# A hybrid decoder step on one core: parameters made earlier, tables on two engines, gates and norms interleaved with other work

## The chip, the cores and the metric

The kernel runs on one core of a Trainium2 chip. The metric is the device time of one execution in microseconds (us), lower is better; the time given is the median of several executions. TensorE (PE), VectorE (DVE), ScalarE (ACT), GpSimd (POOL) and SyncE (SP) each take their instructions in program order from a queue of their own and wait for each other through semaphores. SP here only issues DMA transfers.

## The reference, cut to what matters

One layer of a decoder with two mixers in parallel, for 2048 prompt tokens and 64 sample tokens (8 sequences of 8) that have 4096 past positions in pages.

```python
proj = rmsnorm(x, g_pre) @ w_in            # q, k, v, index queries and keys, index weights, u
# attention: each query attends to the 256 keys with the highest index score
s = einsum('bqhd,bld->bqhl', qi, ki) * 64 ** -0.5
score = einsum('bqhl,bqh->bql', relu(s), wi) * 4 ** -0.5
_, idx = lax.top_k(score, 256)
a_o = sparse_attend(q, take(k, idx), take(v, idx), valid)
# state space: 32 groups of 64 complex states, 16 channels each
dt = exp(log_dt); mag = exp(lr * dt)
ar, ai = mag * cos(li * dt), mag * sin(li * dt)      # decay a
h[t] = a * h[t - 1] + B(a) u[t]                      # a scan over time
y = Re(C h) + d_skip * u
z = gelu(y)
s_o = z * sigmoid(z @ w_glu + b_glu)                 # the GLU gates
# both joined, then the MLP
mix = concatenate([a_o, s_o]) @ w_out
x = x + rmsnorm(mix, g_post)
hdn = square(relu(rmsnorm(x, g_ffn_pre) @ w_up))
y = x + rmsnorm(hdn @ w_down, g_ffn_post)
```

The model's width is 1024, the hidden width 4096. All is fp32. The large products are made as three products of high and low parts.

## The kernel before, in words

The tokens form 17 tiles of 128: 16 of the prompt, one with the 64 sample tokens. The kernel has three stages, `project_inputs` (line 57), `state_space` (384) and `blend` (777). A stage begins when all engines have ended the one before.

**Projections.** For each tile ACT squares and splits x, PE makes four banks of 24 matmuls and the transposes of queries and keys, ACT evacuates them (L192 to L206), DVE and POOL turn them by their positions (L262 to L272, L287 to L295), and SP loads the next tile and stores the last. SP's loads of a tile stand ahead of its stores.

**State space.** SP issues ten parameter loads (L463 to L465), the page table (L466) and u (L459), then gathers pages of index keys into a dense buffer kidx_d (L452): 64 pages before the MT moves and 64 after them; POOL gathers the other 128. Each gather is one load of a page number into a register and one DMA. DVE makes the decay, its sine and cosine with ACT's functions, then three tables by complex products (L373 to L380, seven operations each): eight powers of B, nine of C, and T, the powers of the per-chunk decay, by doubling (L607 to L634). A chunk is 8 tokens, so that the scan runs over 272 columns. PE's banks come in a written order: the eight transposes of the B table (L727), eight banks KT (L734) that need both tables, 24 transposes of u (L742), 32 banks w (L749), 32 banks Y (L756 to L761), and 20 gates (L768). ACT evacuates each bank (L525). DVE regroups u for the transposes (L645, three copies) and adds to KT (L639). SP moves KT into the Toeplitz matrix MT by eight DMAs (L476) when KT is whole, loads the states h0 (L479), and goes on gathering. DVE scans (L662 to L684) in four parts, two halves of the groups by two parts of the tokens; each writes H, which the Y banks need. GELU(y) leaves as four transfers to yt_d (L484) and comes back in another order by 32 (L487), is multiplied by the gates on DVE (L707) and stored as so_d (L492).

**Blend.** All that is left is cut into units, and one list `plan` gives their order for all engines at once. The selection of keys (units S), attention (A), and the samples' part (SQ, SI, SF, SC, SS, SE, SV, SO) come from functions that give each unit a cost; `merge` puts a side list between the units of a main one in proportion to the costs. SF are the 32 steps of the samples' search for the 256th highest score: each compares 4104 scores with a trial, the upper half on DVE (L2160), the lower on ACT (L1817). Four groups g of 4, 4, 4 and 5 tiles then go through the feed units:

- W(g, h, i): the half h of the output projection of tile i (L1433), 
- M1(g, i) and M2(g, i): the two norms behind it, N(g, i) the transposes (L1441),
- U(g, j): the MLP's 16 upward banks (L1455), D(g, m, q): its downward banks (L1470), E(g): the last norm of all tiles of the group.

A norm is a chain: ACT squares and sums (L1668), DVE makes the mean (L1990), ACT the root (L1673), DVE the inverse by one Newton step (L46 to L54) and the scaling by it (L2007, L2014, L2020), POOL adds the residual (L1891, L1902), SP stores or loads tiles in DRAM (L1284, L1296, L1301). In M1 and M2 it runs for one tile at a time; in E all squares come first, one root for all, then all scalings. The two halves of a downward sum are added on ACT and POOL (`act`: L1710, L1876) or DVE (`dve`). The residual tiles of E are loaded (L1296) into the buffer of the upward weights and downward hidden values, UP, which the last D bank still reads, so that these loads wait for all D banks. Search and attention of group g+1 lie beside the feed units of group g; group 3 has nothing beside it.

```python
queued = [u for u in feed if u[0] not in ("M1", "M2")]
...
sum_by[key] = "act" if i % 2 or beside_search(u) else "dve"
```

## Time and profile before

| what | value |
| --- | --- |
| median of 3 executions | 4224.88 us |
| fastest and slowest of them | 4220.42 and 4229.5 us |
| the profiled execution | 4228.36 us |
| its span in the profile | 4226.6 us |
| PE busy | 3284.0 us, 78% |
| PE's weight loads | 2492.9 us, 59% |
| DVE busy | 2168.2 us, 51% |
| ACT busy | 1818.0 us, 43% |
| POOL busy | 1197.2 us, 28% |
| DMA traffic | 357.41 MB, mean 85 GB/s |
| chain of waits | PE 45%, DVE 17%, issue 9%, ACT 6%, POOL 3%, DMA 2% |

The profile is of one execution. Its span runs from the first to the last instruction; the execution's own time is a little longer. A busy time is the time in which an engine computed; issuing DMAs isn't counted. PEclk is the granted clock of TensorE as a share of full speed, where 0.50 is 1.2 GHz and 1.00 is 2.4 GHz; the engine also shows 0.50 where it has nothing to do. DMA is the busy share of the core's 16 DMA engines. The profile divides the time of a view by groups of instructions with the same line, engine and tiles: out<-in, their number, their busy time, the mean or the least, median and greatest duration in ns, and the idle time before them with what ended it. The chain of waits follows the work that ended last back in time.

The stages lie at 0 to 361 us (projections), 361 to 709 (state space), and 709 to 4226.6 (blend). In the blend, 800 to 920 is the samples' search, and the norms of the four groups lie at 1270 to 1367, 1945 to 2128, 2760 to 2941 and 3610 to 3718.

### The profile page before, as it was taken

How to read it: one execution, taken by the hardware profiler on the slowest of the kernel's cores; microseconds unless marked ns; L12 is line 12 of the kernel's file. 1: busy time of each engine (PE TensorE's matmuls, PEld its weight loads, DVE VectorE, ACT ScalarE, POOL GpSimd, SP SyncE). 2: the span in 40 equal slices, each digit the busy share in tenths (PEclk: the TensorE clock that was granted, in tenths of full speed). 3: DMA queues.
4: the chain of work that ended last, by engine and by line, in shares of the span. 5: the costliest groups of instructions: out<-in, count | busy, mean ns of one | idle time of the engine just before them, and what ended most of it. 6: DMA issues, size and time to landing. Idle time of an engine off the chain costs nothing.

```text
span 4226.6 us, 48124 instructions
## 1 busy us (share of the span) xinstructions
PE 3284.0 (78%) x15896; PEld 2492.9 (59%) x15896; DVE 2168.2 (51%) x4234; ACT 1818.0 (43%) x3043; POOL 1197.2 (28%) x1080
## 2 busy tenths in 40 slices
PE   7993535306774899987489999874899999789997
PEld 6882422103453677764367776642677778578886
DVE  4335661593236784347886333577783333533233
ACT  3221211541344654465564445755644444423332
POOL 1222400103200461145034113531471112234344
PEclk9996667657776999998789999986999999889998
DMA  4444245305422222112222111231231111422221
GB/s 143 133 135 133 57 90 144 110 1 152 136 72 87 72 86 75 50 63 95 88 86 81 57 38 53 76 123 54 79 98 51 53 36 50 168 75 75 65 75 68
DMA packets 180516, 357.41 MB, mean 85 GB/s; under 512 B 39051, under 2 KB 93581, under 8 KB 178317
## 3 DMA queue, kind: packets, MB, share of 16 engines
q1 hardware_dynamic: 170028, 333.35, 25.2%
q0 software_dynamic: 10240, 20.99, 1.7%
q8 instruction: 128, 2.10, 0.2%
q14 instruction: 120, 0.98, 0.1%
HBM read 294.44 MB, written 67.01 MB: 86 GB/s over the span
## 4 chain that ended last, share of the span: by engine, by line
PE 45%; DVE 17%; issue 9%; ACT 6%; POOL 3%; DMA 2%; SPq 2%; POOLq 0%; ACTq 0%; DVEq 0%
PE r L1455 13%; PE r L1470 12%; PE po L1519 6%; PE tr L1510 3%; PE sc L1498 3%; DVE junk_v_b L2097 2%; DVE trial_b L2049 2%; PE r L1433 2%; DVE up_b L1950 2%; POOL acc_b L1876 2%; DVE dn_b L1950 2%; PE sc L1497 1%; ACT junk_a_b L1757 1%; ACT hr_b L1668 1%; DVE score_b L2033 1%
## 5 line engine op out<-in xcount | busy, mean ns | idle before, releaser
L1470 PE MATMUL r<-dn_b,h_b 128*128 128x512 f32 x2880 | 747.6, 414 | 103.1 <-ACT part_b L1710 48.2
L1470 PEld LDWEIGHTS r<-dn_b,h_b 128*128 128x128 f32 x2880 | 558.8, 199 | 266.5 <-ACT part_b L1710 63.4
L1455 PE MATMUL r<-x_hi_b,up_b 128*128 128x512 f32 x2048 | 662.6, 397 | 13.9 <-DVE x_lo_b L1970 9.6
L1876 POOL TENSOR_TENSOR acc_b<-acc_b,part_b 128x512 f32<-128x512 f32 x358 | 496.3, 1406 | 559.5 <-ACT part_b L1710 559.4
L1757 ACT ACTIVATE junk_a_b<-score_b,trial_b 128x384 int8<-128x384 f32 (+13 forms) x266 | 348.0, 1308 | 367.5 <-DVE trial_b L2049 350.6
L1455 PEld LDWEIGHTS r<-x_hi_b,up_b 128*128 128x128 f32 x2048 | 390.0, 190 | 105.3 <-issue 12.1
L1455 PE MATMUL r<-x_lo_b,up_b 128*128 128x512 f32 x1024 | 403.2, 394 | 0.0
L1857 POOL TENSOR_TENSOR hr_b<-hr_b 128x512 f32<-128x512 f32 x128 | 142.2, 1111 | 835.1 <-ACT hr_b L1697 835.1
L1786 ACT ACTIVATE pT_b<-tr 128x512 f32<-128x512 f32 (+3 forms) x320 | 168.9, 528 | 392.3 <-PE tr L1510 392.1
L1710 ACT ACTIVATE part_b<-r 128x512 f32<-128x512 f32 x358 | 206.6, 593 | 260.8 <-PE r L1470 172.3
L1519 PE MATMUL po<-V_sb,pT_b 128*128 128x64 f32 x2176 | 314.0, 285 | 3.0 <-DVE o_b L2114 2.3
L1519 PEld LDWEIGHTS po<-V_sb,pT_b 128*128 128x128 f32 x2176 | 272.2, 194 | 68.1 <-issue 54.8
L2128 DVE CUSTOM_DVE_ANT_0 prob_b<-sc,mk_b,mx_b 128x512 f32<-128x512 f32 (+3 forms) x192 | 124.9, 651 | 351.6 <-PE sc L1498 351.0
L1950 DVE TENSOR_TENSOR dn_b<-raw_b,dn_b 128x1024 fp32r<-128x1024 f32 x120 | 167.1, 1392 | 267.0 <-ACT dn_b L1657 266.4
L1950 DVE TENSOR_TENSOR up_b<-raw_b,up_b 128x1024 fp32r<-128x1024 f32 x136 | 190.3, 1400 | 215.0 <-ACT up_b L1657 214.6
L2097 DVE TENSOR_SCALAR_CACHE_REDUCE junk_v_b<-score_b,trial_b 128x384 bf16<-128x384 f32 (+13 forms) x182 | 267.9, 1472 | 1.4
L1865 POOL TENSOR_TENSOR h_b<-hr_b,h_b 128x512 fp32r<-128x512 f32 x128 | 224.2, 1751 | 149.1 <-ACT h_b L1721 149.1
L1455 PEld LDWEIGHTS r<-x_lo_b,up_b 128*128 128x128 f32 x1024 | 195.5, 191 | 38.9
L1792 ACT ACTIVATE prob_b<-prob_b,nmx_b 128x128 f32<-128x128 f32 (+15 forms) x128 | 153.9, 1203 | 139.9 <-DVE nmx_b L2134 139.9
L2128 DVE CUSTOM_DVE_ANT_0 prob_b<-sc,mk_b 128x512 f32<-128x512 f32 (+3 forms) x128 | 82.1, 641 | 241.2 <-PE sc L1498 230.3
L2049 DVE SCALAR_TENSOR_TENSOR trial_b<-trial_b,turn_b 128x1 int32<-128x1 int32 x434 | 183.3, 422 | 15.0
L1581 PE MATMUL r<-kv_b,qz_b 128*64 128x512 f32 x128 | 51.4, 891 | 178.0 <-DVE sbest_b L2189 157.3
(369 smaller groups left out, 6063.5 us busy)
## 6 DMA issues: line engine op xcount, KB each, us to landing
raw_b<-w_up SPq DMA_DIRECT2D x128, 512.0 KB, 3.9
raw_b<-w_down SPq DMA_DIRECT2D x128, 512.0 KB, 3.6
kv_b<-kv_pages SPq DMA_DIRECT2D x128, 128.0 KB, 2.9
kv_b<-kv_pages POOLq DMA_DIRECT2D x128, 128.0 KB, 3.0
raw_b<-w_out SPq DMA_DIRECT2D x64, 256.0 KB, 2.9
x_tok_sb<-x_all SPq DMA_DIRECT2D x17, 512.0 KB, 4.0
xT_sb<-xT_all SPq DMA_DIRECT2D x17, 512.0 KB, 4.6
kic_b<-kidx_d SPq DMA_DIRECT2D x4, 2048.0 KB, 13.7
```

What stands on the lines that cost most here:

```text
L1455: mm = pe.matmul(x[:, 0:w], wt[:, c], y[:, k], start=k == n == 0, stop=(k, n) == (KD - 1, 2))
L1470: mm = pe.matmul(x[:], f[:, tok], w[:, col], start=c == n == 0, stop=(c, n) == (KQ - 1, 2))
L1519: mm = pe.matmul(po[:, h, :], pT[:, prob_no[t, h, b] % 3, k - 4 * b, :], R["V"][:, k, n:n + HD], start=k == 0, stop=k == t)
L1710: act.activation(dst, ring[bank_no[key] % RING][:], ACT.Copy).then_inc(free_act, 1)
L1757: act.activation(junk_a[:, 0:width(t)], score[:, n % 3, 0:width(t)], ACT.Sign, bias=trial[:, 0:1].bitcast(F32), accum_out=count[:, 0:1]).t ...
L1786: act.activation(pT[:, j % 3, 0:m, :], tr[i % 2][:, 0:m * P].rearrange("p (k q) -> p k q", q=P), ACT.Copy).then_inc(tr_free, 1)
L1865: pool.tensor_tensor(z[:, 0:w], s[:, j % 2, :], a[:, 0:w].bitcast(F32), ALU.subtract).then_inc(h_lo_ok, 1)
L1876: pool.tensor_tensor(dst, dst, part[:, add_no[key] % 2, :], ALU.add).then_inc(add_pool, 1)
L1950: dve.tensor_tensor(lo, raw_of(x), hi.bitcast(F32), ALU.subtract).then_inc(lo_ok, 1)
L2049: ins = dve.scalar_tensor_tensor(out=trial[:, new], in0=trial[:, now], scalar=as_int(flip), in1=turn[:, k:k + 1], op0=ALU.bitwise_xor, op1 ...
L2097: c.step(dve.tensor_scalar(junk_v[:, 0:width(t)], score[:, turn_s[t] % 3, 0:width(t)], trial[:, lower_trial(t)].bitcast(F32), 0.0, ALU.is_ ...
L2128: dve.tensor_tensor_reduce(out=prob[:, n % 2, 512 * b:512 * b + w], in0=sc[i % 2][:, 0:w], in1=mk[:, t % 2, 512 * b:512 * b + w], scale=1. ...
```

## The change

It has four parts.

1. **Parameters and pages.** The parameter loads, the page table, exp, sine, cosine and the coefficients are made during the projections: loads at tile 2, ACT's Exp after tile 4, DVE's angles after tile 5, ACT's three functions after tile 6, DVE's coefficients after tile 7. Of the 256 page gathers POOL issues 65 there (five a tile from tile 4 on) and SP 26 (two a tile); the state space keeps 28 on SP before the MT moves, 57 after h0, and 80 on POOL.
2. **State space.** POOL makes the C table, DVE the B table; the complex product has six operations instead of seven and two waits, with four scratch tiles. ACT regroups u by three copies. PE's order becomes: 24 transposes of u, 8 of the B table, 16 banks w, 8 banks KT, 16 banks w, 32 banks Y. The scan of the first half starts behind KT's add and waits for the MT moves only ahead of its first write of H. GELU(y) is stored as z_d by 32 DMAs in its last order, with no read-back; the gates are gone from here.
3. **Start of the blend and gates.** Queries and the first index keys are loaded first, and the keys and values of attention (3.2 MB) after the last load of index keys, at SI(3). The 20 gates become units GL(0) to GL(19), one behind each of SF(1) to SF(20): four matmuls on PE, a sigmoid on ACT, the multiplication on POOL, and stores on SP two gates later. w_glu, b_glu and the first z are loaded at SF(0), into room that the page slots 1 to 6 use later, so the loads of these slots move from SF(1) to SF(6) to SF(22) to SF(27).
4. **Norms by tile.** M1 and M2 of a tile become nine units M(g, i, 0) to M(g, i, 8), E five units E(g, i, 0) to E(g, i, 4) per tile, each one step of one or two engines, and the steps of different tiles are interleaved in the plan. The downward banks go tile by tile, and the second half of each is summed by `act`, the first by `dve` unless search is beside it. The residual loads of E still wait for all D banks.

```diff
...
+                    if t == 2:
+                        for name in par.NAMES:
+                            sp.dma_start(par.tile[name][:], A[name]).then_inc(par.ld, 16)
+                        sp.dma_start(par.pages[:], A["page_table"]).then_inc(par.pages_ld, 16)
                     store_tile(sp, t - 2)
+                    if t >= 4:
+                        par.gather_keys(sp, range(par.AT[1] + 2 * (t - 4), par.AT[1] + 2 * (t - 3)), par.keys_sp)
...
+                    if t == 4:
+                        act.wait_ge(par.ld, 16 * len(par.NAMES))
+                        act.activation(par.S(DT), par.tile["log_dt"][:], ACT.Exp).then_inc(dt_ok, 1)
+                    elif t == 6:
+                        act.wait_ge(angles_ok, 1)
+                        act.activation(par.S(MAG), par.S(X), ACT.Exp).then_inc(trig_ok, 1)
+                        act.activation(par.S(SIN), par.S(RS), ACT.Sin).then_inc(trig_ok, 1)
+                        act.activation(par.S(COS), par.S(RC), ACT.Sin).then_inc(trig_ok, 1)
...
+                    if t == 5:
+                        angles()
+                    elif t == 7:
+                        coefficients()
...
+                    if t >= 4:
+                        par.gather_keys(pool, range(5 * (t - 4), 5 * (t - 3)), par.keys_pool)
...
-def complex_product(dve, c, o_r, o_i, a_r, a_i, b_r, b_i, x, y):
-
-    c.up(dve.tensor_tensor(x, a_r, b_r, ALU.mult))
-    c.up(dve.tensor_tensor(y, a_i, b_i, ALU.mult))
+def complex_product(eng, c, o_r, o_i, a_r, a_i, b_r, b_i, x):
+
+    c.up(eng.tensor_tensor(x[0], a_r, b_r, ALU.mult))
+    c.up(eng.tensor_tensor(x[1], a_i, b_i, ALU.mult))
+    c.up(eng.tensor_tensor(x[2], a_r, b_i, ALU.mult))
+    c.up(eng.tensor_tensor(x[3], a_i, b_r, ALU.mult))
     c.wait()
-    c.step(dve.tensor_tensor(y, x, y, ALU.subtract))
-    c.step(dve.tensor_tensor(x, a_r, b_i, ALU.mult))
-    c.step(dve.tensor_tensor(o_i, a_i, b_r, ALU.mult))
-    c.up(dve.tensor_tensor(o_i, o_i, x, ALU.add))
-    c.up(dve.tensor_copy(o_r, y))
+    c.up(eng.tensor_tensor(o_r, x[0], x[1], ALU.subtract))
+    c.up(eng.tensor_tensor(o_i, x[2], x[3], ALU.add))
     c.wait()
...
+                for t, n in enumerate(CT):
+                    sp.dma_start(U[t][0:n], A["u_d"][AT[t] * CH:(AT[t] + n) * CH, :].rearrange("(n j) c -> n j c", j=CH)).then_inc(u_ld[t], 16)
+                par.gather_keys(sp, range(par.AT[2], par.AT[3]), par.keys_sp)
                 sp.wait_ge(kt_ok, 1)
                 sp.wait_ge(mt_zero, 1)
...
-                gather_keys(sp, (2, 3), keys_sp)
+                par.gather_keys(sp, range(par.AT[3], par.AT[4]), par.keys_sp)
...
+                    for l in range(CH):
+                        sp.dma_start(A["z_d"][f, :, l, :].rearrange("(q c) n -> c q n", c=GC), YT[GC * l:GC * l + GC, 8 * f:8 * f + 8, :]).then_inc(y_st, 16)
...
+                bc = lambda i: sm[:, i, :, None].to_broadcast([P, GP, GC])
+                for l in range(1, CH + 1):
+                    complex_product(pool, c, CAr[:, :, l, :], CAi[:, :, l, :], CAr[:, :, l - 1, :], CAi[:, :, l - 1, :],
+                                    bc(AR), bc(NAI), room(0, 0, GC))
+                pool.memset(sm[:, TH, 0:1], 0.0).then_inc(ca_ok, 1)
+                par.gather_keys(pool, range(par.AT[4], par.AT[5]), par.keys_pool)
...
+                for t, n in enumerate(CT):
+                    act.wait_ge(u_ld[t], 16)
+                    act.activation(Ur[t][0:n].rearrange("p (g j c) -> p j g c", g=G, c=GC), U[t][0:n].rearrange("p j (g c) -> p j g c", c=GC),
+                                   ACT.Copy).then_inc(ur_ok, 1)
...
+                pe.wait_ge(bank_free, BT_END)
+                for v in range(2):
+                    for j in range(HG * v, HG * v + HG):
+                        for BT in (BTr, BTi):
+                            b = bank()
+                            for g in (2 * j, 2 * j + 1):
+                                mm = pe.matmul(b[half(g), 0:NALL], BT[:, j, half(g)], u8[:, g, :], start=True, stop=True)
+                            mm.then_inc(bank_full, 1)
+                    if v == 0:
+                        pe.wait_ge(ca_ok, 1)
+                        for q in range(8):
+                            b = bank()
+                            for i, g in enumerate(range(*of_bank(q).indices(G))):
+                                for k, (BA, CA) in enumerate(((BAr, CAr), (BAi, CAi))):
+                                    mm = pe.matmul(b[0:GC, i * P:(i + 1) * P], BA[half(g), g // 2, CH - 1, :],
+                                                   CA[half(g), g // 2, 0:CH, :], start=k == 0, stop=k == 1)
+                            mm.then_inc(bank_full, 1)
...
 
     def feed_units(g):
         T = nt(g)
-        out = [(("W", g, 0, i), 5.4) for i in range(T)] + [(("W", g, 1, 0), 5.4), (("W", g, 1, 1), 5.4)]
-        for i in range(T):
-            out += [(("M1", g, i), 4.0)]
-            if i + 2 < T and i < 2:
-                out += [(("W", g, 1, i + 2), 5.4)]
-            if i == 1 and T == 5:
-                out += [(("W", g, 1, 4), 5.4)]
-            if i:
-                out += [(("N", g, i - 1), 2.0)]
-            out += [(("M2", g, i), 4.0)]
-        out += [(("N", g, T - 1), 2.0)]
+        out = [(("W", g, 0, i), 5.4) for i in range(T)]
+
+        at = [(2 * i, ("W", g, 1, i), 5.4) for i in range(T)] + [(2 * i + 12, ("N", g, i), 2.0) for i in range(T)]
+        at += [(2 * i + 3 + k, ("M", g, i, k), 0.8) for i in range(T) for k in range(9)]
+        out += [(u, c) for _, u, c in sorted(at, key=lambda x: (x[0], x[1][0] != "W", x[1][2]))]
...
-    plan += merge(first_side[14:], samples[1:]) + [("B",)]
+    for u in merge(first_side[14:], samples[1:]):
+        plan += [u] + [("GL", u[1] - 1)] * (u[0] == "SF" and 1 <= u[1] <= N_GATE)
...
+    is_last = lambda u: u[2] == nt(u[1]) - 1 and u[3] == 0
+    queued = [u for u in feed if u[0] not in "ME" or is_last(u)]
...
-    down_banks = lambda g: [(h, i) for h in range(2) for i in tiles_of(g)]
+    down_banks = lambda g: [(h, i) for i in tiles_of(g) for h in range(2)]
...
-                sum_by[key] = "act" if i % 2 or beside_search(u) else "dve"
+                sum_by[key] = "act" if h or beside_search(u) else "dve"
...
+            elif u[0] == "SF" and N_GATE + 2 <= u[1] < N_GATE + 8:
+                for i in range(2):
+                    eng.wait_ge(so_st[i], 64 * ((len(BLOCKS) + 1 - i) // 2))
+                load_pages(eng, u[1] - N_GATE - 1, b)
...
-                    if kind == "E":
+                    if kind == "E" and is_last(u):
                         sp.wait_ge(ring_full, all_down(g, ND - 1))
...
+                        if u == ("SI", 3):
+                            load_keys()
+                        if u == ("SF", 0):
+                            sp.wait_ge(rl_ok, 2 * NC + 2)
+                            sp.dma_start(wglu[:], A["w_glu"]).then_inc(gl_ld, 16)
+                            sp.dma_start(bglu[:], A["b_glu"]).then_inc(gl_ld, 16)
+                            load_outputs(0)
+                            load_outputs(1)
+                        elif u[0] == "GL":
+                            if u[1] >= 2:
+                                store_gated(u[1] - 2)
+                            if u[1] % 4 == 1 and 2 <= u[1] // 4 + 1 < len(BLOCKS):
+                                load_outputs(u[1] // 4 + 1)
...
+                def gates(k):
+                    i, f = divmod(k, 4)
+                    n = BLOCKS[i][1]
+                    if k == 0:
+                        pe.wait_ge(gl_ld, 32)
+                        pe.wait_ge(rl_ok, 2 * NC + 2)
+                    if f == 0:
+                        pe.wait_ge(z_ld[i % 2], 64 * (i // 2 + 1))
+                    wait(pe, gate_ok, k - 1)
+                    for c in range(4):
+                        mm = pe.matmul(ring[k % 2][:, 0:n * CH], wglu[:, c, f * P:(f + 1) * P], zb[:, i % 2, c, :, 0:n], start=c == 0, stop=c == 3)
+                    mm.then_inc(gl_full, 1)
...
+                    elif u[0] == "GL":
+                        k, m = u[1], BLOCKS[u[1] // 4][1] * CH
+                        act.wait_ge(gl_full, k + 1)
+                        wait(act, so_ok, k - 1)
+                        act.activation(gate[:, k % 2, 0:m], ring[k % 2][:, 0:m], ACT.Sigmoid, bias=bglu[:, k % 4:k % 4 + 1]).then_inc(gate_ok, 1)
...
-                def inverse(u, m):
-                    n = stat_no[u]
-                    s = slice(n, n + m)
-                    dve.wait_ge(ss_ok, n + m)
-                    dve.tensor_scalar(mean[:, s], ssum[:, s], 1.0 / D, EPS, ALU.mult, ALU.add).then_inc(mean_ok, 1)
-                    dve.wait_ge(root_ok, chain_no[u] + 1)
-                    inverse_root(dve, rs[:, s], mean[:, s], root[:, s], newton[:, 0:m], newt, 4 * chain_no[u]).then_inc(rs_ok, 1)
-                    dve.wait_ge(rs_ok, chain_no[u] + 1)
+                def mean_square(u):
+                    x = norm_of(u)
+                    z = slice(col_of[x], col_of[x] + 1)
+                    dve.wait_ge(ss_ok, sq_no[x])
+                    dve.tensor_scalar(mean[:, z], ssum[:, z], 1.0 / D, EPS, ALU.mult, ALU.add).then_inc(mean_ok, 1)
+
+                def scale(u, weight, done):
+                    x, i = norm_of(u), u[2]
+                    z = slice(col_of[x], col_of[x] + 1)
+                    dve.wait_ge(root_ok, root_no[x])
+                    inverse_root(dve, rs[:, z], mean[:, z], root[:, z], newton[:, 0:1], newt, 4 * (rs_no[x] - 1)).then_inc(rs_ok, 1)
+                    dve.wait_ge(rs_ok, rs_no[x])
+                    dve.scalar_tensor_tensor(out=acc(i), in0=acc(i), scalar=rs[:, z], in1=weight, op0=ALU.mult, op1=ALU.mult).then_inc(done, 1)
...
```

## Rows read from the trace of the kernel before

**Rows 1.** The page's first line; busy time by stretch; columns: PE, PEld, DVE, ACT, POOL, PEclk, DMA, GB/s.

```profile
span 4226.6 us, 48124 instructions
...
0.00:361.00 361.00, 319.07 (x1768) 278.95 (x1768) 138.80 (x271) 109.66 (x216) 74.10 (x89) 0.97 0.41 136
...
709.00:747.00 38.00, 0.00 (x0) 0.00 (x0) 0.00 (x0) 0.00 (x0) 0.00 (x0) 0.50 0.95 303
...
1270.00:1367.00 97.00, 40.07 (x137) 26.23 (x136) 64.65 (x198) 49.98 (x104) 9.66 (x5) 0.64 0.24 87
...
1945.00:2128.00 183.00, 95.33 (x320) 64.92 (x320) 147.51 (x298) 103.30 (x171) 44.22 (x24) 0.73 0.28 98
...
2760.00:2941.00 181.00, 96.63 (x309) 63.00 (x307) 147.73 (x254) 101.73 (x154) 39.12 (x21) 0.70 0.26 93
...
3610.00:3718.00 108.00, 67.42 (x282) 53.33 (x281) 55.72 (x109) 40.52 (x79) 25.80 (x11) 0.78 0.39 143
```

**Rows 2.** Timeline of SP in the state space: start, length, operation.

```profile
488.22 14.50 SPq L476 DMA_DIRECT2D MT_sb<-H_sb  x8
...
508.35 80.60 SPq L452 DMA_DIRECT2D kidx_d<-kidxT_pages  x64
...
708.97 0.32 SPq L1367 DMA_DIRECT2D kiT_sb<-kiT_d  x1
```

**Rows 3.** State space: ACT's evacuations of KT and of a gate; W and KT's add.

```profile
L525 ACT ACTIVATE H_sb<-ps x8: 587/587/587, 429.6 to 452.6; 16x512 f32<-16x512 f32 x8
...
652.15 0.69 ACT L525 ACTIVATE Tr_sb<-ps,bglu_sb 128x512 f32<-128x512 f32 x1 [2.75 <-PE ps L768]
...
L749 PE MATMUL ps<-u_sb,mix_sb 128*64 128x272 f32 x128 | 16.5, 424 | 0.3 <-ACT u_sb L525 0.3
...
463.88 0.68 DVE L639 TENSOR_TENSOR H_sb<-H_sb,u_sb 16x512 f32<-16x512 f32 x1
```

**Rows 4.** VectorE and GpSimd alone and beside each other, by form and by line.

```profile
L373 DVE TENSOR_TENSOR u_sb<-CAr_sb,sm_sb 128x256 f32<-128x256 f32 x8 | 3.4, 426 | 0.3
...
L263 DVE TENSOR_TENSOR t_sb<-w_raw_sb,cs_sb 128x320 f32<-128x320 f32 x17 | 19.2, 1128 | 0.0
...
L294 POOL TENSOR_TENSOR qi_sb<-t_sb x17: 872/1543/1553, 52.8 to 342.5; 128x320 f32<-128x320 f32 x17
...
L1902 POOL TENSOR_TENSOR acc_b<-acc_b,up_b x16: 2333/3316/3531, 1993.3 to 4218.0; 128x1024 f32<-128x1024 f32 x16
...
L2020 DVE SCALAR_TENSOR_TENSOR acc_b<-acc_b,rs_b,gbuf_b x16: 1276/1284/3391, 1991.9 to 4209.2; 128x1024 f32<-128x1024 f32 x16
```

**Rows 5.** Timeline of DVE, the scans' first and last writes of H.

```profile
527.76 1.23 DVE L683 TENSOR_TENSOR H_sb<-mix_sb 128x1024 f32<-128x1024 f32 x1
...
589.15 1.21 DVE L684 TENSOR_TENSOR H_sb<-mix_sb 128x1016 f32<-128x1016 f32 x1
```

**Rows 6.** Landing of the four yt_d stores, and the loads of 709 to 747.

```profile
DMA to landing us min/median/max: 4.0/8.9/9.2
...
qi_b<-qi_d SPq DMA_DIRECT2D x2, 128.0 KB, 21.6
```

**Rows 7.** The samples' search, by line.

```profile
L2160 DVE TENSOR_SCALAR_CACHE_REDUCE sjunk_b<-smask_b,strial_b x32: 2328/2329/2330, 799.4 to 915.3; 64x2040 bf16<-64x2040 f32 x32
...
L1817 ACT ACTIVATE sjunk_a_b<-smask_b,strial_b x32: 1999/2014/2016, 800.0 to 915.3; 64x2064 bf16<-64x2064 f32 x32
```

**Rows 8.** What TensorE waited for at group 3's start; chain of waits in its norms.

```profile
PE r L1433 <- DVE h_b L1957: 13.0, 1, 13.0
...
3690.18 2.35 POOL acc_b L1891
...
3699.51 2.36 POOL acc_b L1891
```

**Rows 9.** The tail: timeline of POOL.

```profile
4208.16 12.18 POOL L1902 TENSOR_TENSOR acc_b<-acc_b,up_b 128x1024 f32<-128x1024 f32 x4 [8.78 <-DVE acc_b L2020]
4220.31 2.33 POOL L1902 TENSOR_TENSOR accs_b<-accs_b,xs_b 128x1024 f32<-128x1024 f32 x1
```

539 lines of the change are left out of this document (255 added, 284 removed).

## The prediction

> **What bounds the kernel now.** I read the busy time by stretch first, with cuts where the stages change [rows 1]. The reader is to see which stretches have TensorE (PE) full and which have nobody full. The projections, 0 to 361 us, are PE's: 319 us busy at a granted clock of 0.97. From 709 to 747 every engine stands still while the DMA engines run at 0.95: a load bounds it. The norms between the output projection and the MLP (1270 to 1367, 1945 to 2128, 2760 to 2941, 3610 to 3718) have PE busy for 40, 95, 97 and 67 us of 97, 183, 181 and 108, and VectorE (DVE) for 65, 148, 148 and 56: no engine is full, so hand-overs bound them in part. Second, the timeline of SP shows the state space as one chain of queues: eight MT moves, 64 page loads of 1.26 us each (80.60/64), the yt_d round trip, and the end at 708.97 [rows 2]. Third, single forms give prices [rows 3 to 7], and the chain of waits those of norms and tail [rows 8, 9].
>
> The profiled execution took 4228.36 us, its span 4226.6: 1.8 lie around it. It stands 3.5 above the median, 4224.88. I make the sum against the span, add 1.8 and take off 3.5. A measurement of this kernel can tell 0.2%, 8.4 us, from no change.
>
> **Projections: 0.** Each tile from the fifth on, some 20 us long, gains two page loads on SP (2 x 1.26 us) and five on GpSimd (POOL), 6.3 us at SP's price; POOL is busy 74 of 361 us there [rows 1], so it hides them. The parameters' 50 short DVE operations and ACT's table reloads lie in PE's shadow, since a tile's evacuation has banks in reserve. If that cover is gone at one tile, it costs some 8 us once (the eight parameter loads ahead of a store on SP). I take 0, range 0 to +8.
>
> **State space: -131.** Before, H was first written at 527.76 and last at 590.4, 62.6 us later [rows 5], and the stage ended at 708.97. The new order:
> - U's three loads, each copied by ACT, keep PE in transposes until about 392, my estimate; it decides nothing while the tables last to 410.
> - DVE makes the eight BA products (48 operations of 0.43 us alone for 256 columns) while POOL makes eight CA products (0.87 us alone at 320 columns, so 0.70 at 256). Alone they would take 20 and 34 us. Beside each other they slow down: the DVE form of 320 columns takes 1.13 us where its size suggests 0.53, POOL's 1.54 where it takes 0.87 alone; a 1024-column pair, 1.28 and 2.33 alone, takes 3.32 together [rows 4]. That is 92% of the sum of the two. I take 1.0 us for each of 48 pairs (1.13 alone in sum, less a tenth): 48 us, so both tables are ready at about 410.
> - BT follows to 413, the first half of W (half of PE's 16.5 us [rows 3]) to 421. KT has eight banks; ACT took seven steps in 429.6 to 452.6, 3.3 us each [rows 3], so 27 us: 448. DVE's T table ends at the same time: before, it ran from the first KT bank's start (429.6 - 3.3 = 426) to KT's add at 463.9 [rows 3], 38 us, and 410 + 38 = 448.
> - Then the MT moves: from their first issue at 488.2 to the page loads behind them at 508.4 [rows 2] are 20 us, some 17 to their landing and 3 for h0. So they land at 465; H's first write follows, its last 62.6 later: 528. SP meanwhile has h0 and 57 page loads, 57 x 1.26 = 72 us, from 468 to 540. It is SP, not DVE, that is late next.
> - z_d is then stored directly. Its bytes equal yt_d's, whose stores landed in up to 8.9 us each [rows 6]: 4 x 8.9 = 36, so 577. The read-back and the 20 gates are gone from here.
>
> 709 - 577 = 132; one microsecond is kept for the block's end. Bounds: the stores overlap the page loads' end and the tables hardly disturb each other, -150; the 16-partition stores with 1,088-byte runs at half speed, and a late T, -105.
>
> The rows show a pair of DVE and POOL taking 92% of its sum [rows 4]. The Trainium skill (SBUF — State Buffer, Who interferes with whom) says that a DVE operation with two SBUF inputs and a GpSimd one that reads SBUF contend for one port pair, an exclusive lock. By that rule the pairs cost their full sum, 48 x 1.13 = 54 us instead of 48; by a free overlap 34. The trace is much nearer to the rule.
>
> **Blend's start: -10.** Before PE's first work at 747, 38 us at 303 GB/s move 11.5 MB [rows 1], and qi_b lands 21.6 us after its issue, behind them [rows 6]. The change puts queries and first keys ahead and defers 3.2 MB: 3.2 MB/303 GB/s = 10.6. Bounds 0 and -14. The deferred loads are next needed after the first S units, with PE's index work as cover; without it they cost what they now cost.
>
> **Gates beside the samples' search: +27.** The search is 32 steps, (915.3 - 800.0)/31 = 3.72 us each, of 2.33 on DVE and 2.01 on ACT [rows 7]; PE stands idle. A gate takes PE 3.44 us (0.69 + 2.75) and ACT 0.69 [rows 3]. Both fit the step, just. But ACT's queue is in order: at the first gate it waits for w_glu, z and a first bank. The loads are some 3 MB in small pieces; I take 220 GB/s, under the 303 of [rows 1], so they land 14 us in, at about 814, where the search has only reached its second step; with a first bank of 5.4 us (between 3.44 and twice that) ACT, and DVE behind it, lose 15. Then 20 steps lose 0.6 each (an estimate from the pairs of [rows 4]: DVE beside POOL's 512-column multiply, and ACT's slip): 12. The page loads moved behind the gates, to steps 22 to 27, have the search's last four steps, 15 us, and the ties as cover: nothing; if it is gone, a step or two. Bounds +8 (loads in time) and +80 (below).
>
> **Norms beside the search: -39.** Before, a tile's two norms went ACT, DVE, ACT, DVE, POOL one after another. Split in nine parts and interleaved by tile, other tiles' parts fill the waits. What can be won is bounded by DVE's idle time, 97 - 65 = 32, 183 - 148 = 35 and 181 - 148 = 33 [rows 1]: 100 in all. The number of search units in the same stretches hardly falls (24 to 22, 16 to 15, 13 to 13), three or so more now stand before the next W, and each norm has four more places in the queues. I take under half, 15 + 12 + 12. Bounds 0 and -87.
>
> **Group 3: -20.** No search is left. PE waited 13.0 us for h_b [rows 8], which DVE makes behind the scalings of all the group's tiles. Tile-major sums and per-tile scalings end that, but the third tile's features now wait for SP behind y stores that need POOL's add: 5 of 13 are won. The norms ran at 9.3 us per tile, serially (3690.18 to 3699.51 [rows 8]); pipelined, the pair that bounds it has 0.92 x 4.9 = 4.5 us per tile, POOL's add of 2.35 and DVE's two scalings of 1.28, nearly in turn [rows 4]. Only the last tile's chain then stands behind the last W bank, and the earlier ones overlap: 15 won. Bounds -8 and -30.
>
> **Tail: -3.** POOL's four adds take 12.18 beside DVE, then 2.33 [rows 9]; DVE now finishes earlier, so 5 x 2.33 = 11.7 instead of 14.5. The residual loads still wait for the last D. Bounds 0 and -8.
>
> Sum: -131 - 10 + 27 - 39 - 20 - 3 = -176. 4226.6 - 176 = 4050.6; + 1.8 - 3.5 = 4049.
>
> **Rivals.**
> - *Forecast as above*, 4049: 0.50.
> - *The norms win nothing beside the search.* DVE is 67 to 82% busy there [rows 1] and each part is one more in-order wait. Against: in every one of those rows DVE has 32 us or more left while PE is idle for half the time. 4049 + 39 = 4088: 0.18.
> - *The tables run strictly one after the other*, 54 us, and DVE's T with them. The large pair's 92% speaks for nearly this. 4049 + 6 = 4055: 0.10.
> - *The gates set the search's step.* PE has stood idle since 800, and its granted clock is 0.50, the level of 1.2 GHz, where it idles (709 to 747) [rows 1]. If it stays there in the gates, a gate takes 2 x 3.44 = 6.88 against 3.72, 20 x 3.16 = 63 more. Against: one gate per step keeps PE over 90% busy. 4049 + 63 - 12 = 4100: 0.10.
> - *The norms gain down to DVE's idle time*, -100 instead of -39: 3988: 0.07.
> - *Slower.* The 51 norms of 17 tiles, in 238 parts (17 x 9 M and 17 x 5 E), stand in in-order queues; a part early in one queue holds work behind it on ACT, DVE, POOL and SP, as a D bank's sum behind M's square. To eat 176 and pass 8.4 more, each must cost 184/238 = 0.78 us. It decides from there. For: search units with fixed dues surround them. Against: the waits of other engines that the parts fill are left out of that price. Over 4233, say 4245: 0.03.
> - *The parts that gain are undone by a late load*, near no change: 0.02.
>
> **Range.** The low end takes the rival at 3988; the high end takes in 4100 and the bound of the state space (26 more) only in part: 3985 to 4108. Chances: faster 0.95, the same 0.02, slower 0.03.
>
> **What the changed profile would show.** The first load of the blend's data at 570 to 590 (was 708.97); SP the last engine busy before it, with 57 page loads ending near 540; DVE and POOL both in table products from 362 to 410. PE's next work some 28 us after that first load. One wait of about 15 us on ACT at the first gate, then steps of 3.7 to 4.4 us; 7 would be the cold rival. In each norm stretch, DVE's idle share falls and PE's first U comes 10 to 20 us sooner after the group's last D. POOL's tail 11.7. I am wrong if the state space ends after 605, if the steps take over 5 us, or if the norm stretches are longer than before.

## The result and the profile after

| | before | after |
| --- | --- | --- |
| median of all runs | 4227.19 us | 4072.03 us |
| runs | 4220.42 to 4231.97 (4) | 4068.36 to 4074.11 (4) |
| span of the profiled execution | 4226.6 us | 4070.2 us |

The ratio of the times is 0.9632, its 95% interval 0.9616 to 0.9647: 155 us less. The forecast was 4049, that is 176 less, in a range of 3985 to 4108: the measured time lies in the range, 23 above the forecast.

The page's head of the kernel after, and its busy time by stretch, with cuts at its own stages; columns as in [rows 1]:

```profile
span 4070.2 us, 48292 instructions
...
PE 3275.5 (80%) x15896; PEld 2496.3 (61%) x15896; DVE 2137.9 (53%) x4199; ACT 1834.2 (45%) x3076; POOL 1263.3 (31%) x1181
...
PEclk9998768667778999998699999877899999899998
...
0.00:392.00 392.00, 325.11 (x1768) 282.25 (x1768) 143.31 (x303) 116.10 (x225) 106.39 (x154) 0.96 0.40 134
...
445.00:459.00 14.00, 14.00 (x132) 11.73 (x132) 13.14 (x51) 4.86 (x9) 6.08 (x12) 1.00 0.08 30
459.00:583.00 124.00, 47.70 (x254) 33.63 (x250) 88.37 (x137) 18.74 (x50) 29.40 (x58) 0.68 0.35 80
583.00:609.00 26.00, 0.18 (x2) 0.21 (x4) 0.00 (x0) 0.00 (x0) 0.00 (x0) 0.50 0.88 320
...
661.00:799.00 138.00, 63.77 (x160) 30.04 (x160) 116.10 (x279) 98.34 (x134) 37.69 (x48) 0.72 0.52 127
...
1843.00:1985.00 142.00, 71.07 (x250) 49.88 (x250) 125.16 (x278) 80.06 (x135) 26.15 (x12) 0.70 0.29 104
...
2655.00:2800.00 145.00, 77.36 (x257) 51.88 (x258) 127.53 (x242) 83.45 (x129) 24.29 (x12) 0.70 0.26 92
...
3464.00:3563.00 99.00, 69.44 (x282) 55.46 (x280) 61.91 (x126) 37.45 (x76) 27.19 (x12) 0.79 0.43 154
```

The reader is to see a loss at once: the projections, which ended at 361, now last to 392, with 325 us of TensorE work in them instead of 319. The stretch without any engine, 38 us in [rows 1], is 26 long. The table below has the points at which the kernel passes from stage to stage, from the timelines of both kernels; the last column is what the stage won.

| point | before | after | ahead by | won in the stage |
| --- | --- | --- | --- | --- |
| state space begins | 361.4 | 393.0 | -31.6 | -31.6 |
| blend begins | 709.0 | 582.9 | 126.1 | 157.7 |
| first step of the samples' search | 800.0 | 661.4 | 138.6 | 12.5 |
| first W, group 0 | 1218.4 | 1100.3 | 118.1 | -20.5 |
| first U, group 0 | 1366.7 | 1234.6 | 132.1 | 14.0 |
| W and U, group 1 | 1980.8, 2128.3 | 1843.1, 1984.5 | 137.7, 143.8 | 5.6, 6.1 |
| W and U, group 2 | 2787.4, 2941.4 | 2654.9, 2799.8 | 132.5, 141.6 | -11.3, 9.1 |
| W and U, group 3 | 3610.1, 3717.9 | 3464.2, 3563.4 | 145.9, 154.5 | 4.3, 8.6 |
| last D ends | 4198.8 | 4045.2 | 153.6 | -0.9 |
| end of the span | 4226.6 | 4070.2 | 156.4 | 2.8 |

The timeline of SP in the state space after (before: [rows 2]):

```profile
466.18 11.85 SPq L536 DMA_DIRECT2D MT_sb<-H_sb  x8
480.56 0.64 SPq L539 DMA_DIRECT2D H_sb<-h_re  x1
...
483.29 73.43 SPq L477 DMA_DIRECT2D kidx_d<-kidxT_pages  x57
556.82 21.56 SPq L545 DMA_DIRECT2D z_d<-w_sb  x32
...
582.86 1.35 SPq L1378 DMA_DIRECT2D qid_b<-qi_s_d  x2
```

MT moves begin at 466.2, 73 us into the stage; in the forecast it was 87 (448 of 361). The 57 page loads take 73.4 us and are, as forecast, what ends last; the z stores behind them take 26 us to the blend's first load, not 36.

### The profile page after: what moved, and what is told of

It is laid out like the page before. It is cut to its first block, busy times and chain, and to the rows that moved or that the text cites. A ratio compares the mean times of both kernels' runs of the same rounds, so it can differ in the third digit from the quotient of the medians.

```text
span 4070.2 us, 48292 instructions
## 1 busy us (share of the span) xinstructions
PE 3275.5 (80%) x15896; PEld 2496.3 (61%) x15896; DVE 2137.9 (53%) x4199; ACT 1834.2 (45%) x3076; POOL 1263.3 (31%) x1181
## 4 chain that ended last, share of the span: by engine, by line
PE 47%; DVE 19%; issue 9%; ACT 6%; POOL 2%; SPq 2%; DMA 2%; POOLq 0%; ACTq 0%; DVEq 0%
PE r L1498 14%; PE r L1513 12%; PE po L1562 6%; PE tr L1553 3%; PE sc L1541 3%; DVE junk_v_b L2163 3%; DVE trial_b L2115 3%; PE r L1476 3%; DVE up_b L2019 2%; DVE dn_b L2019 2%; PE sc L1540 2%; ACT junk_a_b L1813 1%; POOL acc_b L1937 1%; DVE acc_b L2067 1%; PE r L1625 1%
## 5 line engine op out<-in xcount | busy, mean ns | idle before, releaser
L1498 PE MATMUL r<-x_hi_b,up_b 128*128 128x512 f32 x2048 | 664.3, 398 | 11.3 <-DVE x_lo_b L2039 10.3
L1937 POOL TENSOR_TENSOR acc_b<-acc_b,part_b 128x512 f32<-128x512 f32 x356 | 485.0, 1381 | 585.6 <-ACT part_b L1771 585.1
L375 PE MATMUL pp<-w_hi_sb,xT_hi_sb 128*128 128x512 f32 (+2 forms) x512 | 179.3, 350 | 25.6 <-ACT w_raw_sb L203 25.5
L1553 PE MATMUL tr<-ident_sb,prob_b 128*128 128x128 f32 x1088 | 177.1, 278 | 7.9 <-ACT prob_b L1848 6.2
```

Of the source, the lines that this page charges most:

```text
L375: mm = pe.matmul(pp[j][:, 0:b - a], x[:, t % 2, k, :], w[:, k, a:b], start=n == 0, stop=n == 3 * KD - 1)
L1498: mm = pe.matmul(x[:, 0:w], wt[:, c], y[:, k], start=k == n == 0, stop=(k, n) == (KD - 1, 2))
L1553: mm = pe.transpose(x[:, (k - 4 * b) * P:(k - 4 * b + 1) * P], prob[:, n % 2, k * P:(k + 1) * P], ident[:])
L1937: pool.tensor_tensor(dst, dst, part[:, add_no[key] % 2, :], ALU.add).then_inc(add_pool, 1)
```

## The experiments

Each kernel is the changed kernel with one edit unless it says otherwise. Times are medians of four executions, unless one execution is named, to be held against 4072.0; intervals are of the ratio to the kernel before, that of the change being 0.9616 to 0.9647. Some intervals overlap or touch: those of the gates, both tables on VectorE, the last norm, the keys and the last residuals that of the change, and at the end those of the sixteen page loads and of the last kernel that of the kernel each builds on. There the times alone don't tell two kernels apart, and the trace has to.

Two differences between the traces aren't the edits'. Kernels with the same projections begin the state space between 392.6 and 396.0 us, so a moment behind it is counted here from its stage's start. And the stretch from group 2's first U to group 3's first W takes 663.5 to 666.2 us in eight of the traces and 658.9 to 659.3 in five, whatever was edited. Here is that place in the kernel after and in the one with the last residuals on VectorE, columns as above. The plan is the same there, and in both TensorE had waited for 8.22 us some 20 us before:

```profile
3040.00:3050.00 10.00, 9.52 (x23) 5.73 (x22) 5.79 (x13) 4.67 (x6) 1.97 (x2) 0.69 0.11 26
```

```profile
3040.00:3050.00 10.00, 9.59 (x41) 6.77 (x40) 5.44 (x12) 5.27 (x7) 3.04 (x2) 1.00 0.23 60
```

The granted clock is 0.69 in one and 1.00 in the other, with 23 and 41 matmuls. Counted from group 2's first U, the two kernels are 1 us apart when they enter this place and 5 behind it. Why the clock falls out one way or the other wasn't tried.

### SP's page loads in the projections, moved by two lines

What TensorE waited for in the first 392 us of the kernel after (line, releaser: us in all, times, longest):

```profile
PE pp L375 <- ACT w_raw_sb L203: 25.5, 11, 6.0
PE pp L387 <- DVE xT_lo_sb L244: 19.0, 1, 19.0
```

The first row is new; it stood at 1.3 us before. The timeline of SP around one tile of the kernel after shows why:

```profile
233.79 0.33 SPq L126 DMA_DIRECT2D qh_d<-qh_sb  x1
...
235.61 0.50 SPq L128 DMA_DIRECT2D qi_d<-qiT_sb  x1
236.90 1.77 SPq L477 DMA_DIRECT2D kidx_d<-kidxT_pages  x2
238.84 0.45 SPq L138 DMA_DIRECT2D x_tok_sb<-x_all  x1
239.34 1.30 SPq L139 DMA_DIRECT2D xT_sb<-xT_all  x1
```

Stores of the turned queries (233.8 to 236.1), the two page loads (236.9 to 238.7), and only then the loads of the next x, for which ACT waits (it began at 245.4). Before, x was loaded 0.6 us after the last of those stores was issued, here 3.2 after. So 2.6 us went into each round, and the rounds grew by nearly all of it: over eleven tiles the first of these stores come 18.4 us apart before and 20.8 after.

```diff
                     load_tile(sp, t)
...
+                    if t >= 4:
+                        par.gather_keys(sp, ...)
                     store_tile(sp, t - 2)
-                    if t >= 4:
-                        par.gather_keys(sp, ...)
```

> The changed kernel, but SyncE issues its two page loads of a projection tile between the load of tile t and the store of tile t-2, where it waits some 10 us anyway, instead of behind the store. Theory: the projections run in a closed loop (SyncE's stores, then the load of the next x, landing, ACT, DVE, the stores again) with under 3 us of slack, and the two page loads (3.0 us with the wait ahead of them) stood in it. Then TensorE's waits on w_raw, 25.5 us, go, the projections end at about 362 to 366 instead of 391, and the time falls by 25 to 29 us to 4043 to 4047. Rival 1: GpSimd's five page loads or the DMA traffic slow the tile; then no more than 5 us change. Rival 2: ACT's table loads do it; then 5 us at most too.

Measured: 4045.6 us (0.9556 to 0.9597), 26.4 less. TensorE's wait there:

```profile
PE pp L375 <- ACT w_raw_sb L203: 5.9, 3, 4.2
```

MT moves now begin at 442.75 instead of 466.18, 23.4 us sooner, and the rounds are 18.9 us. So the two loads' place in SP's loop was the cause of 23 of the 31.6 us. The state space still begins at 369.5, and at 366.4 to 370.9 in the three later kernels with this edit, 5 to 9.5 us later than the 361.4 of before. GpSimd's 65 loads, ACT's table loads and the parameters are all still in place; which of them costs that wasn't tried.

### Gates four steps later

ACT's timeline in the kernel after, around the first gate:

```profile
664.22 2.00 ACT L1873 ACTIVATE sjunk_a_b<-smask_b,strial_b 64x2064 bf16<-64x2064 f32 x1
...
666.33 1.28 ACT L1879 ACT_TABLE_LOAD   x1
680.68 0.69 ACT L1879 ACTIVATE gate_b<-r,bglu_b 128x512 f32<-128x512 f32 x1 [13.06 <-PE r L1668]
...
684.11 0.69 ACT L1879 ACTIVATE gate_b<-r,bglu_b 128x512 f32<-128x512 f32 x1 [0.15 <-PE r L1668]
684.70 2.00 ACT L1873 ACTIVATE sjunk_a_b<-smask_b,strial_b 64x2064 bf16<-64x2064 f32 x1
```

The first gate waited 13.06 us for TensorE, which waited 15.2 for z_d to land; the search's next trial stood behind it.

```diff
-    plan += [u] + [("GL", u[1] - 1)] * (u[0] == "SF" and 1 <= u[1] <= N_GATE)
+    plan += [u] + [("GL", u[1] - 5)] * (u[0] == "SF" and 5 <= u[1] <= N_GATE + 4)
```

with the page loads and the last two stores of the gates four steps later too.

> The changed kernel, but the gates stand behind steps 5 to 24 of the samples' search instead of 1 to 20, and the page loads behind them at steps 26 to 31. Theory: ACT waited 13.1 us (plus 1.3 of a table load) at the first gate for w_glu and z, which land some 14 us after the search's first step; four steps of 3.7 us later they are there. Time falls by 11 to 14 us to 4058 to 4061. Rival: the page loads, now at the search's last steps, land late for the samples' scores and give it back: 0 to -3 us. If the loads were not what ACT waited for, no change and a wait of 13 us at the later gate.

Measured: 4061.2 us (0.9597 to 0.9634), 10.9 less, at the lower end of the forecast. The search, first to last step, by line, after and here:

```profile
L1873 ACT ACTIVATE sjunk_a_b<-smask_b,strial_b x32: 1998/2014/2017, 661.4 to 795.6; 64x2064 bf16<-64x2064 f32 x32
```

```profile
L1873 ACT ACTIVATE sjunk_a_b<-smask_b,strial_b x32: 1998/2015/2017, 664.1 to 787.9; 64x2064 bf16<-64x2064 f32 x32
```

134.2 us have become 123.8, where the search without gates took 115.3 [rows 7]. From the search's first step to group 0's first W it is 427.3 instead of 438.9. ACT still waits 2.5 us for the first gate, as TensorE makes its first bank. So of the 18.9 us that the gates cost the search, 10.4 were the wait for loads. Of the 8.5 that are left, that wait and the table load of 1.3 are up to 3.8, and 20 gates take the other 4.7 or more, some 0.2 to 0.4 us each.

### Both tables on VectorE; one table after the other

```diff
-                for l in range(1, CH + 1):
-                    complex_product(pool, c, CAr[:, :, l, :], CAi[:, :, l, :], CAr[:, :, l - 1, :], CAi[:, :, l - 1, :],
-                                    bc(AR), bc(NAI), room(0, 0, GC))
...
                 dve.wait_ge(ba_ok, 1)
+                for l in range(1, CH + 1):
+                    complex_product(dve, c, CAr[:, :, l, :], CAi[:, :, l, :], CAr[:, :, l - 1, :], CAi[:, :, l - 1, :],
+                                    bc(AR), bc(NAI), room(0, 0, GC))
```

> The changed kernel, but VectorE makes the C table too, behind the B table, and GpSimd only loads pages. Theory: the two engines hinder each other so much (48 pairs took 37 to 38 us, 0.78 each, where VectorE's operation takes 0.43 alone) that two engines win almost nothing: 96 operations of 0.43 are 41 us, so the T table, which bounds the scans' start, begins 4 to 5 us later, at about 434.5 instead of 430. Time +3 to +6 us. Rival, that GpSimd really takes half of the work away: +18 to +20 us. Rival, that the page loads of GpSimd, now 40 us earlier, take load off: 0.

Measured: 4075.6 us (0.9620 to 0.9652), 3.6 more, with intervals that overlap. KT's add, which ends T, comes at 467.95 instead of 465.47, 2.5 us later, but the state space begins 2.8 later in this trace (395.8 instead of 393.0). From the stage's start the add comes at 72.2 instead of 72.5 us, and the stage takes 188.8 instead of 189.9. VectorE makes both tables in 36.9 us (395.8 to 432.7). The third case, that nothing is lost, is what the trace shows, though the reason given for it, the earlier page loads, wasn't tested. For the other test VectorE waits until GpSimd is through:

```diff
+                dve.wait_ge(ca_ok, 1)
                 complex_product(dve, c, BAr[:, :, CH - 1, :], ...)
```

> The changed kernel, but VectorE begins its B table only when GpSimd has ended its C table: neither hinders the other, so the profile gives each price alone. Theory: GpSimd's operation alone takes 0.70 us (48 in 34 us), VectorE's 0.43 (48 in 21), so that the pair beside each other, 0.77 to 0.80, costs 70% of the sum, where I had forecast 90%. The T table ends 17 to 19 us later, time +15 to +20 us, 4087 to 4092. Rival: GpSimd alone takes 0.45 or less, and the pair costs its full sum, as an exclusive lock would have it: the table ends 22 us in, time +5 us.

Measured, one execution: 4085.9 us, 13.9 more, and the MT moves begin 87.3 us into the stage instead of 73.2. GpSimd's products by form, first in the kernel after, then here:

```profile
L447 POOL TENSOR_TENSOR CAi_sb<-H_sb 128x256 f32<-128x256 f32 x8 | 7.1, 884 | 0.0
...
L441 POOL TENSOR_TENSOR H_sb<-CAr_sb,sm_par 128x256 f32<-128x256 f32 x8 | 5.7, 708 | 0.6
```

```profile
L447 POOL TENSOR_TENSOR CAi_sb<-H_sb 128x256 f32<-128x256 f32 x8 | 5.9, 733 | 0.0
...
L441 POOL TENSOR_TENSOR H_sb<-CAr_sb,sm_par 128x256 f32<-128x256 f32 x8 | 5.0, 622 | 0.6
```

And VectorE's, in the same order:

```profile
L447 DVE TENSOR_TENSOR mix_sb<-H_sb 128x256 f32<-128x256 f32 x8 | 6.7, 838 | 0.0
L443 DVE TENSOR_TENSOR H_sb<-mix_sb,sm_par 128x256 f32<-128x256 f32 x7 | 6.6, 946 | 0.0
```

```profile
L447 DVE TENSOR_TENSOR mix_sb<-H_sb 128x256 f32<-128x256 f32 x8 | 3.4, 419 | 0.0
...
L443 DVE TENSOR_TENSOR H_sb<-mix_sb,sm_par 128x256 f32<-128x256 f32 x7 | 2.9, 418 | 0.0
```

Alone, GpSimd's 48 operations ran from 397.4 to 428.8, 31.4 us, and VectorE's from 429.0 to 447.1, 18.1 us. Beside each other they took 36.9 (VectorE, 393.0 to 429.9) and 38.4 us (GpSimd, 394.5 to 432.9). So the pair costs 78% of the sum of 49.5, and VectorE's operations take twice their time: in the 36.9 us of its one table beside GpSimd it makes both without it. The second engine won nothing here, not the 20 us that dividing the work suggests.

### Norms in the old order; only the last norm in the old order

```diff
-        at += [(2 * i + 3 + k, ("M", g, i, k), 0.8) for i in range(T) for k in range(9)]
+        for i in range(T):
+            out += [(("M", g, i, k), 0.8) for k in range(5)]
...
+            out += [(("M", g, i, k), 0.8) for k in range(5, 9)]
...
+        return out + [(("E", g, i, k), 0.8) for k in range(5) for i in range(T)]
```

> The changed kernel with its norm units in the old order: the nine parts of a tile's two norms stand together, tile by tile, with W and N between them as before, and E's parts come step by step (all squares, all means, all roots, all scalings, all adds) behind the last D. The tile-major D banks stay. Theory: interleaving the tiles is what gained, 28 us in groups 0 to 2 and 9 in group 3, so the time rises by 25 to 37 us to 4097 to 4109. Rival: the gain came from the tile-major sums and from a root for each tile in E, or the stretches beside the search are bound by VectorE anyway; then the time rises by under 10 us.

Measured: 4104.4 us (0.9696 to 0.9728), 32.4 more, as forecast. With the second half of the edit alone:

> The changed kernel with only the units E in the old order: all D first, then all squares, all means, all roots, all scalings, all adds; the two norms between output projection and MLP stay interleaved. Of the 32 us that both together cost, this tells E's share. Theory: most is in the norms M, whose stretches fell by 14, 6, 9 and 9 us, while the stretches with E changed by -6, +11 and -4: +0 to +10 us, 4072 to 4082. Rival: E's chain stood ahead of every group's first W (12 to 13 us of wait at group 3): +20 us or more.

Measured: 4085.6 us (0.9641 to 0.9673), 13.6 more: more than I gave E, less than its rival. So, to a few us, the interleaving of E is worth 13.6 and that of M, with E already in the old order, 18.8. Where they win, by TensorE's timeline (W to U is the stretch of M, U to the next W holds E, the last is from the last D's end to the end):

| stretch | before | after | E in the old order | M and E in the old order |
| --- | --- | --- | --- | --- |
| group 0, W to U | 148.3 | 134.3 | 132.7 | 132.9 |
| group 1, W to U | 147.5 | 141.4 | 145.9 | 151.0 |
| group 2, W to U | 154.0 | 144.9 | 156.4 | 159.6 |
| group 3, W to U | 107.8 | 99.2 | 102.6 | 118.0 |
| group 0, U to W | 614.1 | 608.5 | 604.4 | 604.4 |
| group 1, U to W | 659.1 | 670.4 | 664.6 | 659.4 |
| group 2, U to W | 668.7 | 664.4 | 663.8 | 658.9 |
| tail | 27.8 | 25.0 | 31.6 | 31.4 |

In group 0 the order of the norms makes no difference: its stretch is as short in the old order, and what shortened it wasn't tried. In the other groups the interleaved stretch is 9.6, 14.7 and 18.8 us shorter than in the old order, and part of it comes back in the stretch behind it: 4.1 us in group 0 and 11.0 in group 1. Search units that had stood beside the norms now stand there, which is argued, not shown. The 5.5 us of group 2 are the difference of the clock shown above. By whole groups (W to the next W) the interleaved order loses 5.5 us in group 0 and 1.4 in group 1, and wins 9.2 in group 2, 18.8 in group 3's stretch and 6.4 in the tail.

### Keys loaded at once

```diff
+                load_keys()
                 load_index_keys(sp, 1)
...
-                        if u == ("SI", 3):
-                            load_keys()
```

> The changed kernel, but the 3.2 MB of attention keys and values are loaded at the blend's start, ahead of index keys 1 and 2, as before the change; queries and first index keys still come first. Theory: what won 12 us at the start (26 us instead of 38 to TensorE's first work) was what lies ahead of the selection's query qi_b; with the 3.2 MB ahead of it again the time rises by 9 to 12 us to 4081 to 4084. Rival: the order of queries and index keys won it, and the keys ride along: 0 to +3 us.

Measured: 4085.5 us (0.9647 to 0.9680), 13.4 more, a little over the forecast. TensorE's first work comes 38.9 us behind the blend's first load instead of 26.0. So the deferral won all of the 12.5 us that the blend's start won.

### Last residuals on VectorE; a Newton step with one tensor

The timelines of VectorE and GpSimd in the kernel after, at one tile of group 3's norms:

```profile
3534.92 0.16 DVE L50 RECIPROCAL rs_b<-root_b 128x1 f32<-128x1 f32 x1
3535.11 2.31 DVE L52 TENSOR_TENSOR newton_b<-rs_b 128x1 f32<-128x1 f32 x1
3537.45 0.16 DVE L54 TENSOR_TENSOR newton_b<-newton_b,mean_b 128x1 f32<-128x1 f32 x1
```

```profile
3535.02 2.38 POOL L1952 TENSOR_TENSOR acc_b<-acc_b,part_b 128x1024 f32<-128x1024 f32 x1 [2.70 <-DVE acc_b L2067]
```

A product of one number per partition takes 2.31 us, until GpSimd's add is through; its next takes 0.16. That happened at three tiles (3535.1, 3541.7 and 3549.4). A wait of group 3's norms was thus GpSimd's add, in an engine that showed as busy.

```diff
-        at += [(... else max(2 * i + 7, 2 * T + i), ("E", g, i, k), 0.8) ...]
+        at += [(... else max(2 * i + 7, 2 * T + i) + 10 * (T == 5), ("E", g, i, k), 0.8) ...]
...
-                    if kind == "M" and u[3] == 4:
+                    if kind == "M" and u[3] == 4 and g < NG - 1:
...
                         pool.tensor_tensor(acc(i), acc(i), x_in(i), ALU.add).then_inc(res_ok, 1)
...
+                    elif kind in "ME" and u[3] == 4 and g == NG - 1:
...
+                            dve.tensor_tensor(acc(i), acc(i), x_in(i), ALU.add).then_inc(res_ok, 1)
...
+                            dve.tensor_tensor(acc(i), acc(i), z, ALU.add).then_inc(y_ok, 1)
```

The first of these changes, which the expectation below doesn't name, puts the adds of E in group 3 ten places later, behind all of that group's scalings; the two weren't tried apart.

> The changed kernel, but in group 3, where no search is left, VectorE adds the residuals (M's part 4 and E's part 4, ten adds of 128x1024), not GpSimd. Theory: GpSimd's add takes 2.33 us, and a VectorE operation with two inputs in SBUF waits for its end (a Newton step on 128x1 took 2.3 us three times in a row of tiles, where it takes 0.16), so the add costs VectorE 2.1 to 2.3 us anyway, while its own takes 1.23. Group 3's norms get shorter by 3 x 1 to 5 us, and the tail falls from 5 x 2.34 = 11.9 us to 5 x 1.23 = 6.2: together 8 to 11 us less, 4061 to 4064. Rival, that the wait was chance and GpSimd's add really ran beside: the norms get 5 x 1.2 us longer, the tail 5.7 shorter: 0.

Measured: 4056.9 us (0.9581 to 0.9621), 15.2 less, more than forecast. The tail, 25.0 us, is 19.0, the 6.0 that the five adds themselves got shorter. Group 3's W to U is 96.0 instead of 99.2; it is 98.6 to 101.0 in seven other traces with this order of the norms and GpSimd's adds, but 96.6 in that of the next experiment, so these 3.2 aren't safely the edit's. 5.1 more were won ahead of that W, where the edit changes nothing: the difference of the clock shown above. The adds at the end, first after (GpSimd's timeline), then here (the chain of waits):

```profile
4054.40 9.56 POOL L1963 TENSOR_TENSOR acc_b<-acc_b,up_b 128x1024 f32<-128x1024 f32 x4 [5.46 <-DMA xs_b<-x_d]
4063.92 2.34 POOL L1963 TENSOR_TENSOR accs_b<-accs_b,xs_b 128x1024 f32<-128x1024 f32 x1
```

```profile
4047.77 2.27 DVE acc_b L2099 x2
4050.04 1.14 DVE accs_b L2099
```

```diff
-    dve.tensor_tensor(tmp, y, y, ALU.mult)
+    dve.tensor_scalar(tmp, y, y, None, ALU.mult)
```

and so for the other two products of the step.

> The changed kernel, but the three products of the Newton step take their second factor as a scalar of each partition, not as a second tensor. Theory: what waits for GpSimd's add is an operation with two tensors in SBUF; these 128x1 products then never take over 0.2 us (now up to 2.35), and the wait falls on the scaling behind them (two tensors), which shows 2.5 to 3.5 us instead of 1.28. Time -3 to 0 us. Rival: any VectorE operation waits for GpSimd's add; then they still show 2.3 us.

Measured, one execution: 4070.0 us, 2.1 less, which can't be told from no change. The products by line, after and here, and the scaling behind them here:

```profile
L52 DVE TENSOR_TENSOR newton_b<-rs_b x51: 158/159/2327, 1175.0 to 4052.8; 128x1 f32<-128x1 f32 x51
```

```profile
L52 DVE TENSOR_SCALAR newton_b<-rs_b x51: 212/214/217, 1174.9 to 4050.6; 128x1 f32<-128x1 f32 x51
```

```profile
L2067 DVE SCALAR_TENSOR_TENSOR acc_b<-acc_b,rs_b,raw_b x16: 1283/1286/2457, 1196.4 to 3554.5; 128x1024 f32<-128x1024 f32 x16
```

No product ever takes over 0.22 us now, and the scaling with two tensors, at most 1.29 us in the kernel after at this line, waits in its place, up to 2.46. The Trainium skill (SBUF — State Buffer, Who interferes with whom) has the same rule, that an operation of VectorE with at most one SBUF input, outside the modes that use both of its port pairs, doesn't contend with GpSimd. These runs agree: 0.21 us in all 51 cases.

### Sixteen page loads to GpSimd, and all mends together

```diff
-    AT = (0, 5 * (NT - 4), 7 * (NT - 4), 7 * (NT - 4) + 28, 176, DECB * NPAGE)
+    AT = (0, 5 * (NT - 4), 7 * (NT - 4), 7 * (NT - 4) + 28, 160, DECB * NPAGE)
```

on top of the first experiment (sixteen loads; the label's twelve is a slip).

> As e1_pages_early, and of SyncE's 57 page loads behind h0 sixteen go to GpSimd (41 and 96). Theory: SyncE is what ends the state space last (page loads to 532.0, then 21.5 us of z stores, while VectorE ends at 524 and TensorE's last Y bank at about 539); with 16 x 1.27 = 20 us less, the z stores begin at VectorE's end and the last ones wait for the Y banks: 8 us less, 4037 to 4040. Rival: the last Y bank and the landing bound it already: 0 to -3 us. GpSimd's loads, 96 x 1.2 us from 410, end at 525 and do not bound.

Measured: 4038.1 us (0.9537 to 0.9570), 7.5 under the 4045.6 without it. The intervals overlap, but the trace shows the state space 9.1 us shorter, 179.3 instead of 188.4. Then all of it, and the first half of the z stores no longer behind the last scan:

> A kernel with the three mends together: SyncE's page loads early in the tile, sixteen page loads moved from SyncE to GpSimd with the first two groups of z stores not waiting for the last scan, and the gates four steps later. If they are independent: 26 + 11 + 8 = 45 us less, 4025 to 4030. Rival: a gain is given back where the next wait stands ready, above all the z stores that land later than the last Y bank: 4035 or more.

Measured: 4026.9 us (0.9503 to 0.9535), 45.1 under the changed kernel, where 26.4, 10.9 and 7.5 are 44.8: the gains add up. The earlier z stores have no part in it. They begin 142.5 us into the state space instead of 153.1, and the stage takes 180.6 instead of 179.3. With group 3's adds on VectorE as well:

> e8_all_three with group 3's residual adds on VectorE as well. If independent: 8 to 11 us under e8's 4026.9, 4016 to 4019. Rival: as in e9, nothing.

Measured: 4021.5 us (4012.7 to 4027.6; 0.9492 to 0.9544), 5.4 under it, and the intervals overlap. By the traces the tail falls from 25.0 to 19.0, as with the last residuals alone, and group 3's W to U hardly (98.6 to 98.1): what the fourth mend surely wins is the tail's 6.0. This is the fastest version, 206 us under the kernel before and 51 under the change.

## Why the prediction was right, and where not

The direction and the range held; the size was 21 us too large. The time, 4072, lies between the forecast and the rival at 4088, by which the norms win nothing; that rival is out by its mechanism, as they won 27.8 us. That the time came so near the forecast is in part luck: the two largest misses, 31.6 us lost in the projections and 26.7 more won in the state space, nearly cancel, and so the blend's first load, too, fell into the forecast's 570 to 590 (582.9). By its own steps (won, in us, from the table of points above):

| step | forecast | measured |
| --- | --- | --- |
| projections | 0 | -31.6 |
| state space | 131 | 157.7 |
| blend's start | 10 | 12.5 |
| gates beside the search | -27 | -20.5 |
| norms beside the search, to group 3's W | 39 | 27.8 |
| group 3 | 20 | 8.6 |
| last D and tail | 3 | 1.9 |
| sum | 176 | 156.4 |

**Projections.** The step that failed is "I take 0, range 0 to +8". I priced the two page loads rightly (2.5 us, and 2.6 went into each round) and hid them behind TensorE, which was full. But that row (319 us busy of 361) says only that TensorE hardly waited, not how near it was to waiting. SP's loads of the next x stand behind its stores in a loop that feeds TensorE. With 2.6 us more in it a round grew by 2.4, of which 1.9 went again with the loads elsewhere: a slack of under 1 us, my estimate from these three numbers, in each of thirteen tiles. The price of "if that cover is gone" was one tile's, where the cover goes at every tile. The prediction has no row for the slack. The first experiment shows this for 23 of the 31.6 us; the rest stays open.

**State space.** The mechanism was right, with SP's queue last. Its 157.7 us are read from the timelines alone, as no run puts the parameters, the pages or the gates back into the stage. Four terms were too dear. The tables took 40 us (393.0 to 432.9), not 48: the pairs took 0.77 us, not 1.0, since a pair of 256 columns overlaps more (78% of the sum) than the one of 1024 columns whose 92% I took. From the tables to KT's add it was 33 us, not 38. There KT's banks took 13.7 us, not 27, so DVE's T table alone set the end. Before, their granted clock was 0.50, behind a wait of 17.06 us; after W they ran at 1.00 (445 to 459 above). The kernel before:

```profile
426.00:454.00 28.00, 26.60 (x128) 18.08 (x128) 24.88 (x119) 4.70 (x8) 12.66 (x26) 0.50 0.18 55
```

From the first MT move to the page loads it was 17 us, not 20, and the z stores took 26 instead of 36 with their 16 partitions. Together the four make 26 of the 26.7 us. The rival of a strictly exclusive pair, full sum, is out for this shape: by it the tables would have ended at 393 + 50 = 443 instead of 433.

**Gates.** The first gate's stall was 13.1 and a table load 1.3, for 15; the steps lost the other 4.5 of the search's 18.9 us, for 12. The cold rival is out: the granted clock was 0.66 from 675 to 680, at the first bank, and 1.00 from 680 to 700, and the first sigmoids stand 3.43 us apart (680.68, 684.11), as before the change.

**Norms.** 27.8 of 39. The sum of group 1 (W to W, 806.6 before, 811.8 after) got longer, where I had forecast 12 less. The table of the norm experiment shows a part of why the hand-overs were priced too high: of what one stretch wins, some is lost again in the next (11.0 us in group 1). That search units which moved there are the reason is argued, not shown. **Group 3** won 8.6 and not 20. The wait for h_b, of which I gave 5 of 13 us, fell to 10.7, and the pipelined norms stood behind GpSimd's adds:

```profile
PE r L1484 <- DVE acc_b L2067: 14.9, 4, 5.8
PE r L1476 <- DVE h_b L2026: 10.7, 1, 10.7
```

I had counted the pair of scaling and add (4.5 us a tile) and not that a product of the Newton step waits in full for the add as well. GpSimd's adds there begin at 3525.52, 3529.91, 3535.02, 3541.61 and 3549.37, so a tile takes 4.4 to 7.8 us. How much of the missing 9 us that wait is, no run shows: with the scalar factor it moved to the scaling, and without GpSimd's adds the stretch got at most 3 us shorter. What remains open: why group 0's stretch is shorter in either order, the 5 to 9.5 us that the projections keep without SP's loads in the loop, and what decides the clock between group 2's first U and group 3's first W.

## What to carry to other kernels

A full engine hides what is added to another queue only up to that queue's slack per round: find the loop that feeds the full engine (load, landing, conversion, store, next load) and count the slack in it, and put additions where that queue waits anyway. When work is given to GpSimd beside VectorE, take the pair's price from a shape of the same size; here the second engine won nothing of a possible 20 us. Count a moment from the start of its stage before calling it later, since an earlier stage may differ by as much. A gain from interleaving beside other queued work is worth what the whole period gets shorter by, not the stretch.

## What the runs showed of the hardware that I had not expected

A VectorE product of 128x1 takes 0.16 us, or up to 2.33 us when a GpSimd add of 128x1024 is running; with its second factor as a scalar of each partition it took 0.21 and never waited. VectorE and GpSimd products of 128x256 (0.42 and 0.62 to 0.73 us alone) take 0.73 to 0.95 and 0.71 to 0.88 beside each other. VectorE alone makes 96 such products in the 36.9 us that its 48 take beside GpSimd's. The same eight KT banks took 27 us where TensorE had stood idle before (clock 0.50 throughout) and 13.7 behind other matmuls (clock 1.00). And kernels with the same plan were granted 0.69 or 1.00 at the same place behind a wait of 8.22 us, 5 us of difference.
